# Attention probabilities turned by VectorE and transfers instead of TensorE, in a two-layer hybrid decoder trunk on one core

## The reference

```python
xn = rms_norm(x, norm_mix_g[l])
xa, q, k, v, zc, xd = jnp.split(xn @ w_in[l], splits, axis=-1)
s_own = jnp.einsum('bhqd,bhkd->bhqk', rope(q), rope(k)) * HEAD_DIM ** -0.5
s_own = jnp.where(k_pos[None, :] <= q_pos[:, None], s_own, NEG)
p = jax.nn.softmax(s_own, axis=-1)
yb = jnp.einsum('bhqk,bhkd->bhqd', p, v)
...
merged = sum(gates[:, :, b] * (y_b @ w_proj_b[l]) for b in range(4))   # A, B, C, D
x = x + merged @ w_o[l]
hn = rms_norm(x, norm_ffn_g[l])
gu = hn @ w_ffn_in[l]
x = x + (silu(gu[..., :FF_DIM]) * gu[..., FF_DIM:]) @ w_ffn_out[l]
```

## Time and profile before

| | |
|---|---|
| median of 3 runs | 797.4 us (797.38 to 797.59) |
| profiled execution | 797.46 us, span 795.7 us |
| TensorE busy | 788.1 us, 99% of the span |
| VectorE busy | 618.3 us, 78% |
| ScalarE busy | 436.6 us, 55% |
| GpSimd busy | 146.8 us, 18% |
| transfers | 152.23 MB, 191 GB/s in the mean |

### The profile page before, as it was taken

One profiled execution on the slowest core, in us unless ns is written; L12 is line 12 of the kernel. 1 busy time (PEld: TensorE's weight loads), 2 busy tenths in 40 slices (PEclk: granted clock), 3 DMA queues, 4 the chain that ended last, 5 costly groups with the idle time before them and its releaser, 6 DMA issues.

```text
span 795.7 us, 15715 instructions
## 1 busy us (share of the span) xinstructions
PE 788.1 (99%) x6567; PEld 765.4 (96%) x6567; DVE 618.3 (78%) x761; ACT 436.6 (55%) x568; POOL 146.8 (18%) x148
## 2 busy tenths in 40 slices
PE   8999999999999999999999999999999999999997
PEld 8999999999999999999999999999999999999996
DVE  6899999776886766575698899988678767676764
ACT  6766887544654353434465678765356444434434
POOL 2415763074000000000000466513300000000000
PEclk9999999999999999999999999999999999999999
DMA  9975555456645666646568555544646465656541
GB/s 296 306 242 170 182 172 177 159 170 234 219 144 184 208 207 209 209 163 211 170 201 266 159 168 185 180 160 159 212 159 212 160 204 181 218 195 205 185 159 53
DMA packets 118187, 152.23 MB, mean 191 GB/s; under 512 B 3904, under 2 KB 101778, under 8 KB 118128
## 3 DMA queue, kind: packets, MB, share of 16 engines
q1 hardware_dynamic: 116592, 149.30, 57.7%
q0 software_dynamic: 1360, 1.82, 0.8%
q10 hardware_dynamic: 176, 0.27, 0.1%
HBM read 148.23 MB, written 1.05 MB: 188 GB/s over the span
## 4 chain that ended last, share of the span: by engine, by line
PE 99%; DMA 0%; DVE 0%; ACT 0%; issue 0%; DVEq 0%; ACTq 0%
PE bank L974 28%; PE bank L975 28%; PE bank L976 28%; PE bank L1062 3%; PE bank L1064 3%; PE bank L1065 3%; PE bank L1036 1%; PE bank L1035 1%; PE bank L1034 1%; PE bank L1196 1%; PE bank L1176 1%; PE bank L1022 0%; PE bank L1021 0%; PE bank L1023 0%; PE bank L1152 0%; PE bank L1148 0%
## 5 line engine op out<-in xcount | busy, mean ns | idle before, releaser
L974 PE MATMUL bank<-act,w_hi 128*128 128x256 f32 x1472 | 408.5, 278 | 1.0 <-DVE w_lo L1752 1.0
L975 PE MATMUL bank<-act,w_hi 128*128 128x256 f32 x1472 | 406.6, 276 | 0.0
L976 PE MATMUL bank<-act,w_lo 128*128 128x256 f32 x1472 | 406.6, 276 | 0.0
L1400 DVE TENSOR_TENSOR w_lo<-raw,w_hi 128x2048 fp32r<-128x2048 f32 x135 | 315.4, 2338 | 101.9 <-ACT w_hi L648 100.9
L648 ACT ACTIVATE w_hi<-raw 128x2048 fp32r<-128x2048 f32 (+3 forms) x146 | 265.2, 1824 | 133.4 <-PE bank L976 105.7
L974 PEld LDWEIGHTS bank<-act,w_hi 128*128 128x128 f32 x1472 | 276.4, 188 | 2.2 <-issue 1.7
L975 PEld LDWEIGHTS bank<-act,w_hi 128*128 128x128 f32 x1472 | 276.4, 188 | 0.5
L976 PEld LDWEIGHTS bank<-act,w_lo 128*128 128x128 f32 x1472 | 276.4, 188 | 0.0
L974 PE MATMUL bank<-y_hi,w_hi 128*128 128x256 f32 x288 | 79.7, 277 | 0.0
L976 PE MATMUL bank<-y_hi,w_lo 128*128 128x256 f32 x288 | 79.5, 276 | 0.0
L975 PE MATMUL bank<-y_lo,w_hi 128*128 128x256 f32 x288 | 79.5, 276 | 0.0
(11 more groups left out here) (248 smaller groups left out, 996.0 us busy)
## 6 DMA issues: line engine op xcount, KB each, us to landing
raw<-in_w_ffn_in SPq DMA_DIRECT2D x44, 1024.0 KB, 5.0
raw<-in_w_gate SPq DMA_DIRECT2D x32, 1024.0 KB, 5.3
raw<-in_w_ffn_out SPq DMA_DIRECT2D x22, 1024.0 KB, 4.8
raw<-in_w_in SPq DMA_DIRECT2D x18, 1024.0 KB, 6.7
raw<-in_w_o SPq DMA_DIRECT2D x8, 1024.0 KB, 5.0
raw<-in_w_proj_b SPq DMA_DIRECT2D x4, 1024.0 KB, 4.8
raw<-in_w_in SPq DMA_DIRECT2D x12, 256.0 KB, 5.9
gates<-qk SPq DMA_DIRECT2D x32, 64.0 KB, 5.7
```

What stands on the lines that cost most here:

```text
L974: nc.tensor.matmul(o, whi, ahi, start=first, stop=False, skip_group_check=skip)
L975: nc.tensor.matmul(o, whi, alo, start=False, stop=False, skip_group_check=skip)
L976: return nc.tensor.matmul(o, wlo, ahi, start=False, stop=last, skip_group_check=skip)
L1400: V.tensor_tensor(lo, raw[slot][:, :], hi.bitcast(F32), ALU.subtract).then_inc(lo_ready[slot], 1)
```

## The change

The six transposes of a head pair on TensorE, and ScalarE's two copies out of the banks, are taken out. ScalarE now writes the probabilities in an order in which the 32-column blocks of both heads lie side by side (`head_blocks`). Two units after the scores VectorE transposes the whole 128x768 tile in 32x32 blocks with one instruction. Right behind the load of unit ATT + 7, SyncE moves the 16 groups of blocks to the partitions where they belong, each 32 partitions by 768 bytes (`move_blocks`). TensorE reads the result in runs of 32 columns. The units are set anew: scores at 10, 12, 14, 17 (were 10, 13, 16, 19), values at 17, 17, 22, 22 (were 16, 19, 21, 22), pool at 14 (was 13), and the convolution's taps are distributed otherwise. The turned blocks and the four `probsT` lie in tiles that are free at that time; two groups of transfers wait for that.

```diff
-ATT = (10, 13, 16, 19)
-PT_AT = (13, 16, 19, 21)
-PV_AT = (16, 19, 21, 22)
-PV_BANK = (3, 2, 4, 6)
-FOLD_AT, POOL_AT, POOL_BANK = 10, 13, 0
+ATT = (10, 12, 14, 17)
+PV_AT = (17, 17, 22, 22)
+PV_BANK = (3, 0, 4, 6)
+PT_DMAS = 16
+FOLD_AT, POOL_AT, POOL_BANK = 10, 14, 0
...
-TAPS = {7: 1, 9: 1, 11: 2, 12: 2, 13: 1, 14: 4, 15: 3, 16: 3, 17: 4, 18: 4, 19: 3, 20: 3}
+TAPS = {7: 1, 9: 1, 11: 2, 12: 1, 13: 3, 14: 1, 15: 4, 16: 3, 17: 3, 18: 4, 19: 4, 20: 4}
-ACT_TAPS = {7: 4, 8: 4, 9: 2, 10: 2, 13: 4, 14: 3, 15: 3, 16: 3, 17: 3, 18: 3}
+ACT_TAPS = {7: 4, 8: 4, 9: 2, 10: 2, 13: 3, 14: 2, 15: 3, 16: 4, 17: 3, 18: 4}
...
+            def move_blocks(l, hp):
+                sp.wait_ge(blocks_turned, l * HP + hp + 1)
+                if hp == 1:
+                    sp.wait_ge(pooled_ready, l + 1)
+                if hp == 3:
+                    sp.wait_ge(pv_done, l * HP + 1)
+                for b in range(4):
+                    for a in range(4):
+                        sp.dma_start(probsT[hp][32 * b:32 * b + 32, 192 * a:192 * a + 192],
+                                     turned[hp % 2][32 * a:32 * a + 32, 192 * b:192 * b + 192]).then_inc(pt_in[hp], 16)
...
+                    if u - 7 in ATT:
+                        move_blocks(l, ATT.index(u - 7))
...
-                if u in PT_AT:
-                    hp = PT_AT.index(u)
-                    for i in range(2):
-                        act.wait_ge(pt_done, l * 2 * HP + 2 * hp + i + 1)
-                        copy(probsT[:, i, :], bank[6 + i][:, 0:3 * P]).then_inc(bank_free[6 + i], 1)
...
+                    pe.wait_ge(pt_in[hp], 16 * PT_DMAS * (l + 1))
                     for i in range(2):
...
-                        nc.tensor.matmul(o[:, 0:S], v_sb[:, 0, c0:c0 + HEAD_DIM], probsT[:, i, 0:2 * P],
+                        keys, c0 = head_blocks(probsT[hp], i), (2 * hp + i) * HEAD_DIM
+                        nc.tensor.matmul(o[:, 0:S], v_sb[:, 0, c0:c0 + HEAD_DIM], keys[:, 0:2, :, :],
...
-                        for c in range(3):
-                            last = nc.tensor.transpose(bank[6 + i][:, c * P:(c + 1) * P], probs[:, i, c * P:(c + 1) * P],
-                                                       ident[:, :])
...
+                if u - 2 in ATT:
+                    hp = ATT.index(u - 2)
+                    dve.wait_ge(probs_ready, l * HP + hp + 1)
+                    if l or hp > 1:
+                        dve.wait_ge(pt_in[(hp + 2) % HP], 16 * PT_DMAS * (l + (hp > 1)))
+                    V.transpose(turned[hp % 2], probs).then_inc(blocks_turned, 1)
```

More of the change, by code:

```diff
@@ L132 @@
 BANKS[5] = ["S0", "S1", "S2", "S3", "cT1", "cT2", "C", "D"]
-BANKS[6] = ["R1", "par", "wsT", "PT0", "PT1", "PT2", "PT3", "PV3", "C", "D"]
-BANKS[7] = ["stat1", "F", "PT0", "PT1", "PT2", "PT3", "C", "D"]
-TAPS = {7: 1, 9: 1, 11: 2, 12: 2, 13: 1, 14: 4, 15: 3, 16: 3, 17: 4, 18: 4, 19: 3, 20: 3}
+BANKS[6] = ["R1", "par", "wsT", "PV3", "C", "D"]
+BANKS[7] = ["stat1", "F", "C", "D"]
+TAPS = {7: 1, 9: 1, 11: 2, 12: 1, 13: 3, 14: 1, 15: 4, 16: 3, 17: 3, 18: 4, 19: 4, 20: 4}
 POOL_TAPS_FIRST = 8
 CONV_BUFS = 4
-ACT_TAPS = {7: 4, 8: 4, 9: 2, 10: 2, 13: 4, 14: 3, 15: 3, 16: 3, 17: 3, 18: 3}
+ACT_TAPS = {7: 4, 8: 4, 9: 2, 10: 2, 13: 3, 14: 2, 15: 3, 16: 4, 17: 3, 18: 4}
 ROWS = {"pool_scale": (0, 2), "conv_b": (2, 2), "conv_norm_g": (4, 2), "conv_norm_b": (6, 2), "conv_w": (8, 62),
@@ L202, in build @@
         rms_b = sb("rms_b", [P, 1, S])
-        cos_r = sb("cos_r", [P, 1, S])
-        sin_r = sb("sin_r", [P, 1, S])
+        trig = sb("trig", [P, 3, S])
+        cos_r, sin_r = trig[:, 0:1, :], trig[:, 1:2, :]
+        diag = trig[:, 2, :].rearrange("p (t s) -> p t s", t=TT)
         def part(owner, a, shape):
@@ L216, in build @@
         swish_t, glu_t = conv_a, yd_f
-        probs = part(sq[:, :, :], 0, [2, 3 * P])
-        probsT = part(sq[:, :, :], 6 * P, [2, 3 * P])
+        probs = part(sq[:, :, :], 0, [6 * P])
+        turned = [part(trig[:, :, :], 0, [6 * P]), part(gates[:, 26:29, :], 0, [6 * P])]
+        probsT = [part(sq[:, :, :], 6 * P, [6 * P]), part(gates[:, 8:11, :], 0, [6 * P]),
+                  part(gates[:, 29:32, :], 0, [6 * P]), part(sq[:, :, :], 6 * P, [6 * P])]
         conv_n = part(sq[:, :, :], 12 * P, [TT, 256])
@@ L259, in build @@
         rms_t = sb("rms_t", [P, TT])
-        diag = sb("diag", [P, TT, P])
         bn6 = sb("bn6", [P, TT, 6])
@@ L322, in build @@
         probs_ready = sem("probs_ready")
-        pt_done = sem("pt_done")
+        blocks_turned = sem("blocks_turned")
+        pt_in = [sem(f"pt_in{hp}") for hp in range(HP)]
         pv_done = sem("pv_done")
@@ L384, in kview, with head_blocks @@
             return t[:, :].rearrange("p (k n) -> p k n", n=UC)
+        def head_blocks(t, i):
+            return t.rearrange("p (b c i k) -> p i c b k", c=3, i=2, k=32)[:, i, :, :, :]
         def low(b):
@@ L778, in misc @@
                     copy(y_hi[:, 0:2, :], ya_f).then_inc(yhi_ready, 1)
-                if u in PV_AT:
-                    hp = PV_AT.index(u)
+                for hp in [hp for hp in range(HP) if PV_AT[hp] == u]:
                     act.wait_ge(pv_done, l * HP + hp + 1)
                     copy(y_hi[:, 2 + hp, :], bank[PV_BANK[hp]][:, 0:S]).then_inc(yhi_ready, 1)
-                if u in PT_AT:
-                    hp = PT_AT.index(u)
-                    for i in range(2):
-                        act.wait_ge(pt_done, l * 2 * HP + 2 * hp + i + 1)
-                        copy(probsT[:, i, :], bank[6 + i][:, 0:3 * P]).then_inc(bank_free[6 + i], 1)
                 if u in ATT:
@@ L791, in misc @@
                     for i in range(2):
-                        for q, (a, b) in enumerate(((0, P), (P, 3 * P))):
+                        scores = bank[4 + i][:, 0:3 * P].rearrange("p (c b k) -> p c b k", c=3, k=32)
+                        for q, cs in enumerate((slice(0, 1), slice(1, 3))):
                             c = 2 * q + i
-                            last = nc.scalar.activation(probs[:, i, a:b], bank[4 + i][:, a:b], ACT.Exp, scale=SCALE,
-                                                        bias=nmx[:, c:c + 1], accum_out=den[:, c:c + 1])
+                            last = nc.scalar.activation(head_blocks(probs, i)[:, cs, :, :], scores[:, cs, :, :], ACT.Exp,
+                                                        scale=SCALE, bias=nmx[:, c:c + 1], accum_out=den[:, c:c + 1])
                         last.then_inc(bank_free[4 + i], 1)
@@ L800, in misc @@
                     for i in range(2):
-                        for q, (a, b) in enumerate(((0, P), (P, 3 * P))):
+                        for q, cs in enumerate((slice(0, 1), slice(1, 3))):
                             c = 2 * q + i
-                            last = nc.scalar.activation(probs[:, i, a:b], probs[:, i, a:b], ACT.Copy,
-                                                        scale=rden[:, c:c + 1])
+                            o = head_blocks(probs, i)[:, cs, :, :]
+                            last = nc.scalar.activation(o, o, ACT.Copy, scale=rden[:, c:c + 1])
                     last.then_inc(probs_ready, 1)
@@ L1166, in misc @@
                     last.then_inc(f_done, 1)
-                if u in PV_AT:
-                    hp, b = PV_AT.index(u), PV_BANK[PV_AT.index(u)]
+                for hp in [hp for hp in range(HP) if PV_AT[hp] == u]:
+                    b = PV_BANK[hp]
                     bank_wait(l, b, f"PV{hp}")
+                    pe.wait_ge(pt_in[hp], 16 * PT_DMAS * (l + 1))
                     for i in range(2):
-                        pe.wait_ge(bank_free[6 + i], free_at(l, 6 + i, f"PT{hp}", True))
                         o = bank[b][64 * i:64 * i + 64, :]
-                        c0 = (2 * hp + i) * HEAD_DIM
-                        nc.tensor.matmul(o[:, 0:S], v_sb[:, 0, c0:c0 + HEAD_DIM], probsT[:, i, 0:2 * P],
+                        keys, c0 = head_blocks(probsT[hp], i), (2 * hp + i) * HEAD_DIM
+                        nc.tensor.matmul(o[:, 0:S], v_sb[:, 0, c0:c0 + HEAD_DIM], keys[:, 0:2, :, :],
                                          start=True, stop=False, skip_group_check=True)
-                        last = nc.tensor.matmul(o[:, P:S], v_sb[:, 1, c0:c0 + HEAD_DIM], probsT[:, i, 2 * P:3 * P],
+                        last = nc.tensor.matmul(o[:, P:S], v_sb[:, 1, c0:c0 + HEAD_DIM], keys[:, 2, :, :],
                                                 start=False, stop=True, skip_group_check=True)
@@ L1189, in misc @@
                     turn_conv(l)
[L1190 to L1194, removed]
-                        for c in range(3):
-                            last = nc.tensor.transpose(bank[6 + i][:, c * P:(c + 1) * P], probs[:, i, c * P:(c + 1) * P],
-                                                       ident[:, :])
-                        last.then_inc(pt_done, 1)
                 if u == 22:
```

## The result

The changed kernel takes 791.98 us (median of 6 runs, 791.91 to 792.25), the kernel before 797.44 beside it: a ratio of 0.9931 with the interval 0.9921 to 0.9942, so 5.5 us faster. The profiled execution has a span of 790.2 us, 5.5 less than before.

A forecast was written before the change was run, and what follows sets the result against it. TensorE was taken as the bound, busy in 99% of the span and 99% of the chain. 797.46 - 4.9 (transposes removed) + 0.5 (stall) = 793.1 us, with an 8-in-10 range of 792.2 to 797.0.

The forecast's parts named there:

- a stall of 0.5: TensorE waiting for VectorE's last convolution tap at unit 21's stop: 0.45 us in layer 0, 0.05 in layer 1.
- Removed from TensorE: Six transposes a group gone from TensorE's stops, 0.61 us each for 8 groups: 4.9 us saved (4.6 to 5.05).
- Where that lands: At the convolution's turn, unit 21: TensorE at 138.48, VectorE's last tap at 138.9; stalls of together 0.5 us.
- Added to VectorE: One 128x768 transpose a head pair on VectorE, 0.95 us each (0.90 to 1.20).
- the factor of 1.24: VectorE's split subtractions take 2.28 or 2.83 us; that spread set the transpose's high end of 1.20 us.
- Value matmuls: TensorE's value matmuls reading probabilities in runs of 32 elements: taken as 0 extra, 6.5 us if doubled.
- rival (c): Short runs slow the value matmuls: 799.6 if doubled, 793.8 for a tenth; chance of losing over 1 us 0.06.
- SyncE's queue: Sixteen transfers a head pair at 0.63 us an issue, 10.1 us, the last landing 3.6 later; hidden from TensorE.
- rival (b): SyncE's transfers come too late for pair 3's values: 799.0 at 0.89 us an issue; chance 0.14 (0.06 slower than before).
- 32p - 22.1: Both layers' stalls in us when each SyncE issue takes p us; slower than before from p = 0.84.
- Loads held back: Weight loads queued behind SyncE's transfers land later, one 1.2 us after its slot is free; costed at nothing.
- Rivals (a) and (d): (a) VectorE becomes the bound, transposes at 1.20 each, 795.1, chance 0.13; (d) something else sets the end, 797.5, chance 0.03.

The follow-up runs named there:

- runs 8 and 9: GpSimd's convolution additions left out, in the changed kernel (792.00 us) and in the kernel before (797.62 us), one execution each.
- Runs 5 and 12: 5: changed kernel, every VectorE transpose done twice, 793.23 us; 12: changed kernel, pair 3's scores at unit 14 and all values at unit 22, 790.93 us.
- run 10: Changed kernel with scores at units 10, 13, 16, 19 as before and pair 1's values at unit 18: 809.78 us, ratio 1.0163.

## Why the prediction was off, step by step

The forecast missed the profiled execution by 793.06 - 791.93 = 1.1 us, and three terms make it up: 0.96 more taken off TensorE than its 4.9, a stall of 0.5 that did not come, and 0.36 given back by the wait at 250 us, on which the sum had no term.

**Removed from TensorE: right in kind, sized too small.** This is the first failed step. 0.61 a group was read off the stops; put back, a group costs 0.64, 5.1 in all. On top the change took away three changes of the array's shape a layer, 0.36, which the step costed at nothing ("scores, values, pool and fold are only moved"). It counted stops, and the number of stops was the same; it should have counted 64-row, 64-column and full-array stretches. Total 2 x 2.93 = 5.9 instead of 4.9. The trace before had a hint: the same six transposes take 0.63 behind values and 0.58 behind other transposes, and the step took the difference for noise. The clear rows came only with the change: a pair's values take 0.81 up to transposes behind them, and 0.70 up to another pair's values (114.75 to 115.45 above). The Trainium skill (TensorEngine Tiling (Array Packing), "Key Properties") says that changing the tiling mode drains TensorE, without a figure. These runs agree that a change costs time, 0.12 to 0.22 us; that a drain is the reason, no row shows.

**Where that lands: mechanism right, size wrong.** The second failed step. No stall of 0.5 came. TensorE arrived at 138.14, 0.34 earlier than forecast (0.07 of it an earlier start of the whole trace, the rest what the first step had too small); VectorE ended at 136.67, 2.2 earlier. Taps and splits took 2.1 us less than before because fewer of them met GpSimd, shown by runs 8 and 9. The transposes start 0.89 to 0.90 ahead of what follows, which is 0.2 less than 4 x 0.95. The waits for TensorE vanished as forecast, but 0.4 for ScalarE's `y_hi` stands in their place. That makes 1.9 of the 2.2; where the last 0.3 went is open. The durations of the trace before were taken as fixed, though the step ahead of it quoted 2.28 and 2.83 for one shape. Runs 5 and 12 show the stall when VectorE is given more or TensorE comes sooner.

**Added to VectorE: right**, 0.97 for 0.95, and the factor of 1.24 kept for the high end never showed. The rule of the Trainium skill (SBUF — State Buffer, "Who interferes with whom") that a one-input instruction keeps clear of GpSimd while one with two inputs may not: both halves agree, 0.97 beside a busy GpSimd, and 0.62 against 0.48 for a tap.

**Value matmuls: right.** Runs of 32 elements cost nothing; rival (c) falls.

**SyncE's queue: no harm, sizes off.** 0.68 to 0.75 an issue for 0.63; in run 10 the group was at 0.63 (10.01 for 16). Landing 3.3 in the median for 3.6. The section of the Trainium skill that rival (b) cites (DMA: Bandwidth & Descriptors, "Anatomy of one DMA") states its fixed 2 us for transfers issued through GpSimd; these are SyncE's, and here the quickest landed after 1.8 us, while sixteen were issued in 10.9 to 12.0. The group that counts most, pair 3's, was the quickest at 0.68, by which rival (b)'s sum, 32p - 22.1, gives no stall; at 0.75 it would give 1.9, but that sum had pair 3's transpose 2.2 us later than it was. Loads held back were costed at nothing, and did cost nothing, but ScalarE's 8.2 us of waits show how near that was.

**Rivals (a) and (d):** VectorE was not the bound, and the saving was not hidden.

Together: 797.46 - 2 x 2.93 + 0.36 (the wait at 250 us) = 791.96, and measured 791.93 in the profiled execution.

What stays open: whether a change into the scores' shape costs another amount than one into the values' (0.12 to 0.22 are means over mixed kinds), why VectorE's instructions meet GpSimd's less often in the changed kernel, and what brings the wait at 250 us, a hundred microseconds behind the changed stretch.

## What to carry to other kernels

Count the changes of TensorE's array shape, not the stops: each costs 0.1 to 0.2 us here, while one more stop in the shape of the products cost 0.01, so group small work by its shape. Before adding up another engine's durations, ask which of them were measured beside a busy GpSimd; an upper and a lower sum (0.48 and 0.62 a tap) would have held the result. A transfer chain replaced TensorE's work for free only because its source was moved up to two units earlier; run 10, with the late sources, lost 12 us against before.

## What the runs showed of the hardware that was not expected

A change between 128*128, 64*128 and 128*64 use of the array: 0.12 to 0.22 us. VectorE's tap of 128x256 with two inputs: 0.48 us alone, 0.62 in the mean of the kernel before. One VectorE transpose of 128x768 in 32x32 blocks: 0.97 us, whether GpSimd is busy or not. In run 10 TensorE was idle for some 6 us; its granted clock was 0.82 in that stretch (145 to 152 us), 0.50 in 152 to 156 and 0.97 in 156 to 160.
